# Branch c of a two-block transformer kernel: scores of four steps into four PSUM banks, value products of eight steps in step 22

## The reference

```python
h = rms_norm_2(x, g_mix[l])
proj = h @ w_in[l]
c_q, c_kv, k_r, qkv_b, qkv_c, gate_logits = jnp.split(proj, IN_SPLITS_2, axis=-1)
y_a = mla_mixer(...)             # 8 heads, softmax over 256 keys
y_b = dilated_mixer(...)         # 12 heads, banded softmax
y_c = neighbourhood_mixer(qkv_c[:, :, 0], qkv_c[:, :, 1], qkv_c[:, :, 2], rpb[l])   # 8 heads of 64
gates = jax.nn.sigmoid(gate_logits).reshape(B, S, N_BRANCH, D_MODEL)
merged = gates[:, :, 0] * (y_a @ w_pa[l]) + gates[:, :, 1] * (y_b @ w_pb[l]) + gates[:, :, 2] * (y_c @ w_pc[l])
x = x + merged @ w_o[l]
x = x + (silu(rms_norm_2(x, g_ffn[l]) @ w1[l]) * (h @ w3[l])) @ w2[l]
```

## Time and profile before

| | us |
|---|---|
| median of three runs | 1535.86 (1535.68 to 1536.5) |
| the profiled execution, its own time | 1535.41 |
| its span, first to last instruction | 1533.7 |
| PE busy | 1522.7 (99%) |
| DVE busy | 1096.0 (71%) |
| ACT busy | 802.2 (52%) |
| POOL busy | 40.1 (3%) |

### The profile page before, as it was taken

One profiled execution on the slowest core, in us unless ns is written; L12 is line 12 of the kernel. 1 busy time (PEld: TensorE's weight loads), 2 busy tenths in 40 slices (PEclk: granted clock), 3 DMA queues, 4 the chain that ended last, 5 costly groups with the idle time before them and its releaser, 6 DMA issues.

```text
span 1533.7 us, 19837 instructions
## 1 busy us (share of the span) xinstructions
PE 1522.7 (99%) x8182; PEld 1293.3 (84%) x8182; DVE 1096.0 (71%) x1374; ACT 802.2 (52%) x948; POOL 40.1 (3%) x36
## 2 busy tenths in 40 slices
PE   9999999999999999999999999999999999999997
PEld 7888888888888888888887888888888887888886
DVE  5778666676786666977757886667877758876666
ACT  6646444456564454765445364544665445464444
POOL 0100000001000000002000100000002000100000
PEclk9999999999999999999999999999999999999999
DMA  9525555554255554445343455554444433555551
GB/s 314 196 106 197 187 197 190 190 193 165 104 199 190 195 192 160 160 147 185 138 151 124 184 196 197 193 178 168 172 156 163 146 123 138 206 206 192 178 203 59
DMA packets 44281, 265.95 MB, mean 173 GB/s; under 512 B 6048, under 2 KB 9248, under 8 KB 14368
## 3 DMA queue, kind: packets, MB, share of 16 engines
q1 hardware_dynamic: 41504, 262.02, 47.7%
q10 hardware_dynamic: 2688, 2.67, 0.7%
HBM read 263.63 MB, written 1.05 MB: 173 GB/s over the span
## 4 chain that ended last, share of the span: by engine, by line
PE 97%; DVE 1%; DMA 0%; SPq 0%; issue 0%; ACT 0%; DVEq 0%
PE psum L578 21%; PE psum L482 18%; PE psum L484 18%; PE psum L483 18%; PE psum L587 11%; PE psum L520 5%; PE psum L959 1%; PE psum L890 1%; PE psum L912 1%; PE psum L950 1%; PE psum L897 1%; DVE wl L1476 1%; DMA raw<-in_weights 0%; PE psum L748 0%; PE psum L732 0%; DVE work L2016 0%
## 5 line engine op out<-in xcount | busy, mean ns | idle before, releaser
L1476 DVE TENSOR_TENSOR wl<-raw,wh 128x2048 fp32r<-128x2048 f32 (+1 forms) x245 | 550.8, 2251 | 220.2 <-ACT wh L1061 220.1
L1061 ACT ACTIVATE wh<-raw 128x2048 fp32r<-128x2048 f32 (+2 forms) x249 | 465.8, 1874 | 320.8 <-PE psum L484 196.2
L482 PE MATMUL psum<-wh,xhl 128*128 128x512 f32 (+2 forms) x928 | 365.6, 394 | 0.5 <-DVE xhl L1704 0.4
L484 PE MATMUL psum<-wh,xhl 128*128 128x512 f32 (+2 forms) x928 | 357.6, 385 | 0.0
L483 PE MATMUL psum<-wl,xhl 128*128 128x512 f32 (+2 forms) x928 | 356.8, 385 | 0.0
L578 PE MATMUL psum<-xhl,wh 128*128 128x512 f32 x1408 | 336.6, 391 | 0.0
L578 PEld LDWEIGHTS psum<-xhl,wh 128*128 128x128 f32 x1408 | 261.2, 188 | 52.3
L482 PEld LDWEIGHTS psum<-wh,xhl 128*128 128x128 f32 x928 | 174.4, 188 | 36.9 <-issue 3.8
L484 PEld LDWEIGHTS psum<-wh,xhl 128*128 128x128 f32 x928 | 174.3, 188 | 34.8
L483 PEld LDWEIGHTS psum<-wl,xhl 128*128 128x128 f32 x928 | 174.6, 188 | 31.6
L587 PEld LDWEIGHTS psum<-xhl,wl 128*128 128x128 f32 x1408 | 175.3, 192 | 3.7
(11 more groups left out here) (196 smaller groups left out, 1236.0 us busy)
## 6 DMA issues: line engine op xcount, KB each, us to landing
raw<-in_weights SPq DMA_DIRECT2D x233, 1024.0 KB, 4.8
raw<-in_weights SPq DMA_DIRECT2D x10, 512.0 KB, 3.8
raw<-in_weights SPq DMA_DIRECT2D x4, 832.0 KB, 4.3
raw<-in_weights SPq DMA_DIRECT2D x12, 256.0 KB, 7.2
work<-in_rpb ACTq DMA_DIRECT2D x4, 438.0 KB, 8.0
raw<-in_weights SPq DMA_DIRECT2D x2, 768.0 KB, 4.2
out<-arena SPq DMA_DIRECT2D x3, 256.0 KB, 3.0
x<-in_x SPq DMA_DIRECT2D x4, 128.0 KB, 3.6
```

The costliest lines, as they stand in the source:

```text
L482: nc.tensor.matmul(dst, lh, right(wh, slot), start=start, stop=False)
L484: return nc.tensor.matmul(dst, ll, right(wh, slot), start=False, stop=stop)
L1061: nc.scalar.activation(wh[:, slot, 0:n], raw[:, slot, 0:n], ACT.Copy).then_inc(high_ready.sem, 1)
L1476: nc.vector.tensor_tensor(wl[:, slot, 0:n], raw[:, slot, 0:n], wh[:, slot, 0:n].bitcast(F32), ALU.subtract).then_inc(split_ready.sem, 1)
```

## The change

- Branch c's turns are now (16, 17), (18, 19), (20, 21), (22, 23): the last two single steps are one turn.
- The scores of two turns are computed at once (`SCORES_AT`): those of turns (16, 17) and (18, 19) behind step 15, those of (20, 21) and (22, 23) behind step 19. The second turn of a pair has banks ACC+2 and ACC+3, and `biased_c` and `prob_c` are two buffers, one for each turn of a pair.
- Where the maximum, exponential and sums of a turn stand on ACT and DVE is set by `SOFTMAX_AT` and the edits of the DVE loop. For the second pair, ACT takes both exponentials in step 19; DVE takes the second row maximum in step 19, behind the sums of the first, and the second sums in step 20.
- The value products of branch c (both halves, 32 matmuls) come in one go behind the transposes in step 22; those behind step 19's half and at the end are gone. The last transposes and copies move from step 23 to step 22, the outputs and their parts to step 23.
- On DVE, the copies of the transposed tiles come before the row maximum in steps 17 to 21 (`MAXIMUM_FIRST` is gone), and the low parts of pieces 35 and 36 are taken in steps 21 and 22, not in step 23.

In the diff, cut to its core:

```diff
-    [(16, 17), (18, 19), (20, 21), (22,), (23,)]
+    [(16, 17), (18, 19), (20, 21), (22, 23)]
-TURN_AT = {m + (m == 1): u for m, u in TURN_ENDING.items()}
-TRANSPOSES_FIRST = range(8, 22)
-MAXIMUM_FIRST = range(17, 23)
+TURN_AT = {m + (m == 1) - (m == 23): u for m, u in TURN_ENDING.items()}
+TRANSPOSES_FIRST = range(8, 24)
+SCORES_AT = {15: (TURN_ENDING[17], TURN_ENDING[19]), 17: (), 19: (TURN_ENDING[21], TURN_ENDING[23]), 21: (), 22: ()}
+SOFTMAX_AT = {15: (TURN_ENDING[17],), 16: (TURN_ENDING[19],), 17: (), 19: (TURN_ENDING[21], TURN_ENDING[23]),
+              21: (), 22: ()}
...
-        biased_c = part(arena, 3072, 1024)
+        biased_c = [part(arena, 3072, 1024), part(arena, 4096, 1024)]
+        prob_c = [part(arena, 5120, 1024), part(arena, 6144, 1024)]
...
-                            mm = nc.tensor.matmul(bank(ACC + hh)[:, (i // 2) * SEQ:(i // 2 + 1) * SEQ],
+                            mm = nc.tensor.matmul(bank(ACC + 2 * pair_in_c(u) + hh)[:, (i // 2) * SEQ:(i // 2 + 1) * SEQ],
...
+                    if last == 15:
+                        pe.wait_ge(*max_ready.by(L, TURN_ENDING[19] + 1))
-                    for m in (last - 2, last) if kind == "b" else range(last - 3, last + 1):
+                    for m in {"a": range(last - 3, last + 1), "b": (last - 2, last), "c": range(16, STEPS)}[kind]:
+                        if m in (22, 23):
+                            pe.wait_ge(*tr_free.by(L, copied + m - 21))
...
                     attend(u)
+                    if m == 22:
+                        weighted(u)
...
-                    scores(u + 1)
+                    for scored in SCORES_AT.get(m, (u + 1,)):
+                        scores(scored)
...
-                weighted(len(TURNS) - 1)
                 project(L, 35, 22, 0)
...
-                    if m in (2, 22):
+                    if m == 2:
                         softmax_exp(TURN_AT[m] + 1)
-                    if m == 22:
+                    if m == STEPS - 1:
+                        act.wait_ge(*o_full.by(L, 5))
+                        nc.scalar.activation(y_t["c"][:, :, 0:P], part(bank(ACC + 2), 0, 4, P), ACT.Copy, scale=0.5)\
+                            .then_inc(o_free.sem, 1)
                         branch_c_high(0)
                     split_high(L, q + 3)
-                    if m + 1 < STEPS and m in TURN_AT and m not in (2, 22):
-                        softmax_exp(TURN_AT[m] + 1)
+                    for u in SOFTMAX_AT.get(m, (TURN_AT[m] + 1,) if m in TURN_AT and m != 2 else ()):
+                        softmax_exp(u)
...
+                    if m == 16:
+                        row_max(TURN_ENDING[19])
                     if u is not None:
-                        if m in MAXIMUM_FIRST and m != 22:
-                            row_max(u + 1)
                         probs_out()
-                        if m not in MAXIMUM_FIRST:
+                        if m < 16 or m == 19:
                             row_max(u + 1)
...
-                    if u is not None:
-                        unit_sums(u + 1)
+                    for softmax in SOFTMAX_AT.get(m, (u + 1,) if u is not None else ())[0:1]:
+                        unit_sums(softmax)
+                    if m == 19:
+                        row_max(TURN_ENDING[23])
+                    if m == 20:
+                        unit_sums(TURN_ENDING[23])
                     if m == 21:
                         split_low_half(L, 34, 1)
+                        split_low(L, 35)
                     if m == 22:
-                        branch_c_low(0)
+                        split_low(L, 36)
```

More of the change, by code:

```diff
@@ L97 @@
     "o_full": (0, 6), "o_free": (0, 6), "bias_in": (0, 32), "bias_ready": (0, 1), "merged_ready": (0, 2), "sum_ready": (0, 2),
-    "dve_step": (26, 54), "act_step": (6, 0),
+    "dve_step": (26, 52), "act_step": (6, 0),
 }
@@ L404, in transposed, with pair_in_c, prob_of @@
                 return prob_t_b[j // 2][:, (j % 2) * 768:(j % 2 + 1) * 768]
-            return part(arena, 5120 + 512 * j, 512) if m >= 20 else prob_t4[j]
+            return part(arena, 7168 + 512 * j, 512) if m >= 20 else prob_t4[j]
         def o_bank(kind, t):
             return bank(ACC + 3 if kind == "b" else ACC + 2 + t)
+        def pair_in_c(u):
+            return step_kind(TURNS[u][0])[2] // 2
+        def prob_of(u):
+            return prob_c[pair_in_c(u)] if step_kind(TURNS[u][0])[0] == "c" else prob
         def heads_of_turn(u):
@@ L924, in probs_t @@
                     else:
-                        blocks = [prob[:, b * P:(b + 1) * P] for b in range(4 * len(TURNS[u]))]
+                        blocks = [prob_of(u)[:, b * P:(b + 1) * P] for b in range(4 * len(TURNS[u]))]
                     for i in tiles or range(len(blocks) // 4):
@@ L990, in turn @@
                         pe.wait_ge(*proj_free[1].by(L, 13))
-                    scores(u + 1)
+                        pe.wait_ge(*o_free.by(L, 3))
+                    if m == 19:
+                        pe.wait_ge(*o_free.by(L, 4))
+                    for scored in SCORES_AT.get(m, (u + 1,)):
+                        scores(scored)
                     if 8 <= m < 16:
@@ L1016, in _ @@
                         pe.wait_ge(*xl_ready.by(L, 9))
-                        project(L, q, 19 + q - 32, 0, between=between, at=(1, 1))
+                        project(L, q, 19 + q - 32, 0)
                     if m == 0:
                         latent_t(TR2["ak_rest"] + 2, ak_tok, (3,))
-                    if m < STEPS - 1 and m in TURN_AT and m != 2:
+                    if m in TURN_AT and m != 2:
                         turn(m)
@@ L1971, in row_max @@
                             rev = part(bias[:, 2 * j + hh, :], at, 4, GRID_W)[:, :, ::-1]
-                            two = part(psum[:, ACC + hh, :], (i // 2) * SEQ, 4, GRID_W)
+                            two = part(psum[:, ACC + 2 * pair_in_c(u) + hh, :], (i // 2) * SEQ, 4, GRID_W)
                             ins = nc.vector.tensor_tensor_reduce(
-                                part(biased_c, i * SEQ, 4, GRID_W), two, rev, 1.0, LOWEST, ALU.add, ALU.max,
+                                part(biased_c[pair_in_c(u)], i * SEQ, 4, GRID_W), two, rev, 1.0, LOWEST, ALU.add, ALU.max,
                                 smax[:, 4 + i:5 + i])
@@ L1987, in unit_sums @@
                     heads = prob_b if kind == "b" else \
-                        [prob[:, i * SEQ:(i + 1) * SEQ] for i in range(2 * len(TURNS[u]))]
+                        [prob_of(u)[:, i * SEQ:(i + 1) * SEQ] for i in range(2 * len(TURNS[u]))]
                     at = 32 + 4 * t + j if kind == "b" else (0 if kind == "a" else 16) + 8 * t + 2 * j
@@ L2090, in _ @@
                         split_low(L, 33)
-                output(5)
-                merge(35, 0, 1, 23, between=lambda: branch_c_low(1))
+                branch_c_low(1)
+                merge(35, 0, 1, 23)
                 split_low(L, 37)
```

31 lines of the change are left out of this document (11 added, 20 removed).

## The result

| | median, us | against before |
|---|---|---|
| before | 1535.88 (4 runs) | |
| changed | 1545.95 (1545.01 to 1546.22, 4 runs) | 1.0064, 95% interval 1.0046 to 1.0081 |

The changed kernel is 10.1 us slower. The forecast was 1546.4 us, with a range of 1542.5 to 1550 and a chance of 0.92 that it would be slower.

The account below looks back on a forecast made before the run. PE, busy 1522.7 of 1533.7 us, bounds the kernel. Per layer, waits of 4.1 + 1.9 + 0.7 = 6.7 less a gain of 1.2 to 1.6, taken as 5.3; both layers +10.6: 1546.4 us, range 1542.5 to 1550.

Parts of the forecast that it names:

- The bound and the place: PE bounds the kernel; tightest before piece 32, where ACT's read of bank PROJ ends 0.14 us ahead of PE.
- PE's gain: Fewer switches between kinds of matmul on PE save about 1.2 us per layer, with 1.0 and 1.6 as ends.
- The products' return to pace: Products interrupted two times fewer, with fewer late first products: 0.4 us per layer, between 0.2 and 0.8.
- the term for POOL's addition: Branch c's outputs reach POOL earlier, so its addition no longer falls beside DVE's split: 5.3 taken, not 5.4, per layer.
- The first wait: Before piece 32, PE waits for ACT's bank read behind the second exponentials: 832.2 against 828.1, 4.1 us.
- The second wait: Before piece 33, PE waits for DVE's first merge of piece 32, which frees the bank: 1.9 us.
- the rival of the clock: Clock falls in the first wait, piece 32 takes 5.6 us; mostly hidden, or costly at 1552 to 1554, chance 0.12.
- The third wait: Within the value products, the last eight wait for DVE's last two copies: 0.7 us.
- The sum: Per layer, 6.7 us of waits less a gain of 1.2 to 1.6; 5.3 taken, +10.6 for both layers.
- The rival of the first wait alone: DVE and ACT catch up after the wait before piece 32: 1541.7 us; chance 0.10, with smaller sums included.
- The rival without waits: ACT's chain is hidden and only PE's gain remains: 1532.7 to 1533.9, say 1533.4 us; chance 0.08.
- The fall of PE's busy time by 13 us: In the changed kernel's profile, PE's busy share was to fall by about 13 us in the span.

Follow-up runs that it names:

- e3_touch: The kernel before with four more unused copies on ACT in step 19, directly ahead of the reads of the gates' banks; 1538.18 us (1.0015).
- e2_both: The changed kernel with ACT's exponentials of turn (22, 23) moved to step 20 and DVE's sums and low-part splits reordered; 1532.46 us (0.9977).
- e5_dve: The changed kernel with only the DVE part of e2_both, ACT as in the changed kernel; 1545.19 us (1.0062).
- e1_act: The changed kernel with ACT's exponentials of turn (22, 23) taken in step 20, not step 19, DVE's order unchanged; 1542.43 us (1.0043).
- e6_halves: e2_both with the value products of steps 16 to 19 taken apart again, behind step 21's transposes; 1535.66 us (0.9999).

## Why the prediction was right

**The bound and the place.** Right. The tightest place was the read of the bank that ends at 827.42. e3_touch shows that it had no slack: 1.23 us put ahead of it cost 1.23 us. The starts even show PE held up a little there before: 0.31 us from the last product of piece 31 to the first of piece 32, where e2_both has no more than the usual 0.23.

**PE's gain.** Right at its edge: forecast 1.2 per layer, with 1.0 and 1.6 as the ends, and e2_both gains 1.6 (67.84 us against 69.47 from branch c's first transposes to those of `merged`). The blocks came out as priced (scores 1.92 for 1.95, value products 3.64 for 3.66), 0.8 in all. The products' return to pace, put at 0.4, gave some 0.8: that is what is left of the 1.6, and of 0.2 that e2_both loses in small waits, behind the 0.8 of the blocks and the 0.2 before the transposes of `merged`. Those 0.2 are the term for POOL's addition, for which the prediction took off 0.1. Before, DVE's split at 852.37, which begins beside that addition (850.68 to 853.08), took 2.86 us and the next one 2.28; in e2_both the addition is over at 851.26 and the split at 851.28 takes 2.29.

**The first wait.** Forecast 4.1 us, from a chain of nine terms; measured 4.15 as idle time in both layers, and 4.3 by the starts (832.62 less 828.08 and one product). The chain's stations came 0.4 us late throughout (second exponentials 828.4 forecast, 828.79 measured), and PE itself 0.2 (it could have had the bank at 828.30, as in e2_both; 828.1 forecast). Most of both is the 0.3 by which branch c's first transposes came later in this execution.

**The second wait.** Forecast 1.9 us. In the trace of the first layer 0.3 of it stand as a wait, in the second nothing. The clock had fallen to 1.2 GHz, and piece 32 took 4.4 us (832.62 to 837.03) and not 2.83. At the high clock PE would have been through with it and the transposes at 836.24 and would have stood until 838.11, by this estimate from the rows 1.9 us; DVE's sums and merge, which set that moment, follow each other without a gap from 834.88. So the wait was sized rightly and was filled by slow products. This is the rival of the clock in its mild form (0.12 had been put on its costly one), in which the second and third waits hide it. That rival put 5.6 us on piece 32; it took 4.4 and 5.0. e5_dve shows both halves of it: without DVE's late chain the second wait goes, and the clock then costs 1.5 to 2.4 us per layer.

**The third wait.** Forecast 0.7, measured 0.56 in the first layer and 0.24 in the second. In the first, PE came 0.3 us later than forecast to the value products, and DVE's last copies, which set the end, began at 844.21 (forecast 844.0).

**The sum.** Forecast +5.3 per layer, measured +5.0 and +5.1. The span's 10.4 us hold 0.3 that this execution had lost before branch c; the medians, 10.1 apart, agree with the smaller figure. The sum held though the second wait was mostly replaced, since it was made from the chain on ACT and DVE and not from PE's waits.

**The rival of the first wait alone** (1541.7) fell with e1_act: take the first wait away, and 3.0 of its 4.2 us stand before the next piece, with a dip of the clock behind them. **The rival without waits** (1533.4) is what e2_both reached, 1532.46, by other orders on ACT and DVE. Its forecast had been given a chance of 0.08 for the kernel as it was.

**What the trace was to show.** The wait of 4 us twice, the second exponentials 5 us behind the first (823.71 and 828.79), and the dip were there. The fall of PE's busy time by 13 us wasn't: it rose by 2.3. That sign was wrong, because the prediction counted its second wait as idle and the slow products that filled it count as busy.

## What to carry to other kernels

When two units of work are put side by side on the engine that bounds the kernel, look at what stands behind the second unit's steps in the other engines' queues: here a read of a bank waited behind exponentials that could not start, while ACT stood idle. Lay the chain out across the engines from rows of the old trace and compare its end with the moment at which the bounding engine comes back; a sum of PE's own gains says nothing of it. When one wait is taken away, expect the next one in the same chain, and move both.

## What the runs showed of the hardware

- The granted clock can fall after the engine has resumed. In the changed kernel's first layer it was 1.00 throughout the wait of 4.15 us and fell within 832 to 834, with the first products at 832.62; in the second it fell within the wait, between 1290 and 1291. In e1_act it fell behind a wait of 3.02 us: the products at 835.08 and 835.85 ran at full pace, those from 836.69 on at half. In e3_touch, with waits of 1.2 us, and in e6_halves, with waits of 1.45, there was no fall.
- How long it stays low differs between two layers of one execution, for the same program text. In e5_dve that made 0.9 us between them.
- A low clock costs nothing where another engine's chain sets the end: 23.38 us in both layers of the changed kernel. The share of busy time hides it as well: PE was busy for 2.3 us more, with the same instructions.
- A group of its own costs about 0.2 us for a change of the kind of matmul: eight score instructions in one group took 1.92 us, in two groups of four 2 x 1.07. The Trainium skill (TensorEngine Tiling (Array Packing), Key Properties) says that such a change drains the engine; the trace agrees in that the group has a fixed price of about this size, and no run here shows what it is made of.
